# Local attention steps between the input projection's matmuls, linear attention levels on half of the queries, and its norm sums as columns

## The reference, cut to what matters

```
attn = sliding_window_attention(aq, ak, av, sinks) * silu(ag)   # 8 query heads, 2 key heads, 64 wide, window 128
rkv  = rkv + (shift(rkv) - rkv) * mu_rkv                        # token mix, 6 tiles of 128 channels
rwkv = rwkv7(h, r, k, v, ...) * silu(rg)                        # 4 heads
# linear attention, 4 heads, 32 keys and 64 values wide; b = cumulative sum of the gate's logs
A[i,j] = sum_d q[i,d] k[j,d] exp(b[i,d] - b[j,d])   for j <= i
o      = A @ v + (q exp(b)) @ S
gla    = o * rsqrt(mean(o*o) + 1e-5) * norm_w * silu(gg)
```

## Time and profile before

| | |
|---|---|
| median of 3 runs (lowest, highest) | 2209.52 us (2199.64, 2214.57) |
| the profiled execution | 2206.71 us, its span 2204.7 us |
| TensorE busy, share of the span | 1927.6 us, 87% |
| VectorE busy | 1241.7 us, 56% |
| ScalarE busy | 638.6 us, 29% |
| GpSimd busy | 103.1 us, 5% |
| mean granted TensorE clock | 0.930 |
| HBM read | 146.59 MB, 67 GB/s over the span |
| the projection's 208 matmuls (L1453) | 181.7 us busy |

### The profile page before, as it was taken

One profiled execution on the slowest core, in us unless ns is written; L12 is line 12 of the kernel. 1 busy time (PEld: TensorE's weight loads), 2 busy tenths in 40 slices (PEclk: granted clock), 3 DMA queues, 4 the chain that ended last, 5 costly groups with the idle time before them and its releaser, 6 DMA issues.

```text
span 2204.7 us, 34977 instructions
## 1 busy us (share of the span) xinstructions
PE 1927.6 (87%) x14866; PEld 1658.0 (75%) x14866; DVE 1241.7 (56%) x2291; ACT 638.6 (29%) x1219; POOL 103.1 (5%) x54
## 2 busy tenths in 40 slices
PE   3999663499799887899999999798889999999997
PEld 1444443395499744799999999498866799999996
DVE  6110247641465566478787334689466558878523
ACT  1011331221321355232222222311167632222221
POOL 0000000020000000000000001033300000000000
PEclk8999875799899988799999999899999999999998
DMA  7333100001044200133332333143200022323331
GB/s 296 119 124 96 38 0 1 0 4 39 29 120 132 58 1 1 39 97 94 89 94 89 96 96 106 29 115 103 73 20 1 1 94 89 94 89 96 89 102 60
DMA packets 51002, 160.68 MB, mean 73 GB/s; under 512 B 7968, under 2 KB 8864, under 8 KB 50720
## 3 DMA queue, kind: packets, MB, share of 16 engines
q1 hardware_dynamic: 43360, 147.62, 21.8%
q10 hardware_dynamic: 7488, 10.82, 1.9%
HBM read 146.59 MB, written 2.10 MB: 67 GB/s over the span
## 4 chain that ended last, share of the span: by engine, by line
PE 78%; DVE 17%; issue 2%; ACT 1%; DMA 1%; ACTq 0%; SPq 0%; DVEq 0%
PE banks L460 16%; PE banks L461 16%; PE banks L462 16%; PE banks L1453 8%; PE banks L1577 3%; PE banks L1739 3%; PE banks L527 2%; DVE arena L1354 2%; DVE top L1353 2%; PE banks L581 1%; PE banks L505 1%; PE banks L517 1%; PE banks L1515 1%; PE banks L553 1%; DVE stat L1117 1%
## 5 line engine op out<-in xcount | busy, mean ns | idle before, releaser
L460 PE MATMUL banks<-hn_hi,w_hi 128*128 128x264 f32 x2288 | 659.3, 288 | 30.5 <-DVE hn_lo L1033 14.2
L461 PE MATMUL banks<-hn_lo,w_hi 128*128 128x264 f32 x2288 | 654.4, 286 | 0.0
L462 PE MATMUL banks<-hn_hi,w_lo 128*128 128x264 f32 x2288 | 653.8, 286 | 0.0
L799 ACT ACTIVATE w_hi<-raw 128x1024 fp32r<-128x1024 f32 x207 | 219.5, 1062 | 895.7 <-PE banks L462 861.3
L460 PEld LDWEIGHTS banks<-hn_hi,w_hi 128*128 128x128 f32 x2288 | 437.1, 191 | 34.9 <-issue 20.3
L461 PEld LDWEIGHTS banks<-hn_lo,w_hi 128*128 128x128 f32 x2288 | 437.7, 191 | 0.1
L462 PEld LDWEIGHTS banks<-hn_hi,w_lo 128*128 128x128 f32 x2288 | 435.3, 190 | 0.0
L1027 DVE TENSOR_TENSOR w_lo<-raw,w_hi 128x1024 fp32r<-128x1024 f32 x181 | 221.6, 1225 | 199.6 <-ACT w_hi L799 199.6
L460 PE MATMUL banks<-a_hi,w_hi 128*128 128x264 f32 x704 | 199.6, 284 | 1.6 <-DVE u_in L1240 1.6
L461 PE MATMUL banks<-a_lo,w_hi 128*128 128x264 f32 x704 | 200.5, 285 | 0.0
L1453 PE MATMUL banks<-hn_raw,ring 128*128 128x512 f32 x416 | 181.7, 598 | 20.6 <-DVE hn_raw L1984 20.6
(11 more groups left out here) (336 smaller groups left out, 2750.9 us busy)
## 6 DMA issues: line engine op xcount, KB each, us to landing
raw<-in_weights SPq DMA_DIRECT2D x207, 512.0 KB, 3.6
ring<-in_weights SPq DMA_DIRECT2D x50, 512.0 KB, 4.2
arena<-arena ACTq DMA_DIRECT2D x144, 66.0 KB, 2.2
arena<-in_gate_w SPq DMA_DIRECT2D x8, 512.0 KB, 4.6
h<-in_xT SPq DMA_DIRECT2D x2, 1024.0 KB, 10.7
out_t<-h SPq DMA_DIRECT2D x4, 512.0 KB, 2.8
arena<-in_alibi SPq DMA_DIRECT2D x1, 1024.0 KB, 5.3
arena<-in_cosT ACTq DMA_DIRECT2D x2, 264.0 KB, 3.2
```

What stands on the lines that cost most here:

```text
L460: mm(o, w[0][:, j, :], x[0][:, k, t], start=first, stop=False)
L461: mm(o, w[0][:, j, :], x[1][:, k, t], start=False, stop=False)
L462: ins_ = mm(o, w[1][:, j, :], x[0][:, k, t], start=False, stop=last)
L799: nc.scalar.activation(w_hi[:, j % SPLIT, :], raw[:, j % RAW, :], ACT.Copy).then_inc(S["w_hi_done"], 1)
```

## The change

It has three parts.

1. **Order of the projection.** The groups come as low-rank inputs, local attention's q, k, v and gate, then the other fourteen: r, k, v of the third mixer (6), q, k, v of linear attention (4), and two pairs of gates. The first 17 items (`ALONE`) use banks as before; the last 14 alternate between banks 4 and 5. Attention starts after item 16, and its 16 steps (transposes(u), scores(u+1), values(u-1)) are issued behind every seventh of the 112 matmuls. ScalarE evacuates the late items between its attention parts, VectorE does a token mix in steps 2 to 7 and a gate sum in steps 8 to 15. The queries are held once; the scores are two products over 64 rows in two banks, the values two products 64 columns wide, and the gate one instruction. The identity and the alibi table are loaded earlier, the casts of two constants come after attention, the remaining gates are copied and get their silu during linear attention's levels.
2. **Levels.** The distances are formed by two instructions of half the length, queries are scaled and multiplied in the later halves alone (256 instead of 512 columns), and one masked copy takes two heads of 256 elements each. The masks come as bytes from memory in the packed order, and the diagonal has its own.
3. **Norm.** Sums, root and reciprocal of linear attention work on 8 columns per tile, and are spread by `spread_columns`.

```diff
-        for g in range(8, N_IN1):
+        for g in range(8, 12):
             in1(g + 5, g)
...
             for s in range(2):
-                last = mm(psum[:, u % 3, s * w:(s + 1) * w], qz1[:, g, s, n * P:(n + 1) * P], k1[:, lo:lo + w], start=True, stop=True)
+                r = slice(64 * s, 64 * s + 64)
+                last = mm(psum[:, 2 * (u % 2) + s, 0:w], q1[r, g, n * P:(n + 1) * P], k1[r, lo:lo + w], start=True, stop=True)
...
+            for b in range(blocks):
+                for s in range(2):
+                    r = slice(64 * s, 64 * s + 64)
+                    last = mm(psum[r, 7, 0:P], v1tok[:, max(0, n - 1) + b, r],
                               pt1[:, u % 2, (s * blocks + b) * P:(s * blocks + b + 1) * P], start=b == 0, stop=b == blocks - 1)
...
+        def s1_step(u):
+            s1_transposes(u)
+            if u + 1 < 16:
+                s1_scores(u + 1)
+            if u >= 1:
+                s1_values(u - 1)
+        s1_scores(0)
+        for g in range(12, N_IN1):
+            def between(k, at=8 * (g - 12)):
+                if (at + k) % 7 == 6:
+                    s1_step((at + k) // 7)
+            in1(g + 5, g, between=between)
         s1_values(15)
...
         s1_exp(0)
         for u in range(16):
+            while 8 * taken + 7 <= 7 * u + 6 and taken < 14:
+                late(taken)
+                taken += 1
+            s1_copy(u)
             if u + 1 < 16:
                 s1_exp(u + 1)
...
         for u in range(16):
+            s1_normalise(u)
             if u + 1 < 16:
                 s1_max(u + 1)
-            s1_normalise(u)
             if u >= 1:
                 s1_gate(u - 1)
+            if 2 <= u < 8:
+                token_mix(u - 2)
+            elif u >= 8:
+                gate_sum(u - 8)
         s1_gate(15)
+        ve.wait_ge(S["consts_in"], 16 * 9)
+        V.tensor_copy(identb[:, :], ident[:, :])
...
-            j = n - S_IN1 - 16
+            j = n - S_IN1 - 20
...
+            V.tensor_tensor(g_half(e, lv, 1), b[:, :, s:2 * s], edge, ALU.subtract)
+            V.tensor_tensor(g_half(e, lv, 0), edge, b[:, :, 0:s], ALU.subtract).then_inc(S["g_diff"], 1)
...
+                    if lv < 7:
+                        o = slice(c * 64, (c + 1) * 64)
+                        last = mm(psum[:, hd, o], g_kl[r, lv % 2, t], g_ql[r, lv % 2, o], start=True, stop=True)
...
+            for hd in range(0, 4, 2):
+                ve.wait_ge(S["g_score"], 4 * lv + hd + 2)
+                if lv < 7:
+                    at = g_at[:, hd:hd + 2, :].rearrange("p h (n a w) -> p h n a w", a=2, w=1 << lv)[:, :, :, 1, :]
+                    shape = [P, 2, T1 // 2]
+                    V.copy_predicated(at, glamask[:, lv:lv + 1, :].to_broadcast(shape).rearrange("p h (n w) -> p h n w", w=1 << lv),
+                                      psum[:, hd:hd + 2, 0:T1 // 2].rearrange("p h (n w) -> p h n w", w=1 << lv)).then_inc(S["g_taken"], 1)
...
+        A(rgate, rgate, ACT.Silu)
+        A(ggate, ggate, ACT.Silu)
...
-            mm(bank(2 + j), bones, g_o_sq(j), start=True, stop=True).then_inc(S["g_osum"], 1)
+            column_sums(psum[:, 2 + j, 0:8], g_o_sq(j)).then_inc(S["g_osum"], 1)
+        for j in range(2):
+            pe.wait_ge(S["g_oinv"], j + 1)
+            spread_columns(bank(4 + j), g_cols[:, 8 * j:8 * j + 8]).then_inc(S["g_orow"], 1)
...
+            V.reciprocal(g_cols[:, 8 * j:8 * j + 8], g_cols[:, 8 * j:8 * j + 8]).then_inc(S["g_oinv"], 1)
```

More of the change, by code:

```diff
@@ L171, in build @@
     att_at = c1.at
-    qz1 = c1.take(4, 2, T1)
+    q1 = c1.take(4, T1)
     k1 = c1.take(T1)
     v1 = c1.take(T1)
+    p1 = c1.take(2, 2, 256)
+    pt1 = c1.take(2, 4 * P)
+    v1tok = c1.take(4, P)
     tail_at = c1.at
@@ L179, in build @@
     dmix = c1.take(T1)
-    mask_in = c1.take(8, P)
     cond = c1.take(D)
@@ L192, in build @@
     g_d = cg.take(2, T1)
-    g_ql = cg.take(2, T1)
+    g_ql = cg.take(2, T1 // 2)
+    g_sq = cg.take(2, T1)
+    g_cols = cg.take(16)
     g_kl = cg.take(2, T1)
@@ L336, in build, with in_bank @@
     ITEMS = 31
+    ALONE = 17
+    def in_bank(item):
+        return bank(item % 8 if item < ALONE else 4 + (item - ALONE) % 2)
     def zb_d(k):
@@ L1452, in in1 @@
                     pe.wait_ge(S["hn_ready"], k + 1)
-                last = mm(bank(item % 8), w[:, k, :], rhs(k), start=k == 0, stop=k == KT - 1 and g > 0)
-            last.then_inc(S["slot_used"], 1)
+                last = mm(in_bank(item), w[:, k, :], rhs(k), start=k == 0, stop=k == KT - 1 and g > 0)
+                if k == KT - 1:
+                    last.then_inc(S["slot_used"], 1)
+                if between:
+                    between(k)
         in1(0, 0)
@@ L1577, in both_heads @@
                 last = mm(out(s), lhs[r], rhs[r], start=start, stop=stop)
[L1578 to L1586, removed]
-            for n in range(4):
-                for s in range(2):
-                    last = mm(out[64 * s:64 * s + 64, n * P:(n + 1) * P], src[:, 2 * n + s:2 * n + s + 1].to_broadcast([P, 64]), ident[:, :],
-                              start=True, stop=True)
             return last
@@ L1800, in _ @@
         evac(glow, 1).then_inc(done, 1)
-        for j in range(6):
+        for j in range(4):
             take(2 + j)
-            evac(zb[:, j, 1:T1 + 1], 2 + j).then_inc(done, 1)
+            evac(q1[:, j, :], 2 + j).then_inc(done, 1)
+        take(6)
+        evac(k1, 6).then_inc(done, 1)
+        take(7)
+        evac(v1, 7).then_inc(done, 1)
         for j in range(2):
@@ L1863, in s1_copy, with late @@
             A(pt1[:, u % 2, 0:w], psum[:, 6, 0:w], ACT.Copy).then_inc(S["s1_pt"], 1)
+        LATE = ([(zb[:, j, 1:T1 + 1], 1.0) for j in range(6)] + [(gq, 32.0 ** -0.5), (gk, 1.0)] + [(gv[:, j, :], 1.0) for j in range(2)]
+                + [(rgate[:, j, :], 1.0) for j in range(2)] + [(ggate[:, j, :], 1.0) for j in range(2)])
+        def late(j):
+            dst, f = LATE[j]
+            take(ALONE + j)
+            evac(dst, ALONE + j, scale=f).then_inc(done, 1)
+        taken = 0
         s1_exp(0)
         for u in range(16):
+            while 8 * taken + 7 <= 7 * u + 6 and taken < 14:
+                late(taken)
+                taken += 1
+            s1_copy(u)
             if u + 1 < 16:
                 s1_exp(u + 1)
-            s1_copy(u)
+        while taken < 14:
+            late(taken)
+            taken += 1
         act.wait_ge(S["g_cum"], 1)
@@ L1992, in _, with token_mix @@
         ve.wait_ge(S["zeroed"], 1)
-        for j in range(6):
-            ve.wait_ge(S["in1_evac"], 3 + j)
+        def token_mix(j):
+            ve.wait_ge(S["in1_evac"], ALONE + 1 + j)
             st.link(V.tensor_tensor(dmix, zb[:, j, 0:T1], zb[:, j, 1:T1 + 1], ALU.subtract))
@@ L2356, in _constants @@
         lvl.append(-1.0 * (((j % 64) // (2 * s) == q64 // (2 * s)) & (j % (2 * s) < s) & (q64 % (2 * s) >= s)))
-    gla = [((j // (2 * s) == q // (2 * s)) & (j % (2 * s) < s) & (q % (2 * s) >= s)) for s in (1 << np.arange(7))]
-    gla.append(j == q)
+    gla = []
+    for n in range(7):
+        s = 1 << n
+        late = q.reshape(-1, 2, s)[:, 1, :].reshape(1, -1)
+        gla.append(np.tile((j // (2 * s) == late // (2 * s)) & (j % (2 * s) < s), (1, 4)))
+    gla = np.stack(gla, axis=1)
     gblock = (i[:, None] // 32 == np.arange(256)[None, :] // 64)
```

154 lines of the change are left out of this document (68 added, 86 removed).

## The result

The changed kernel takes 2134.39 us (median of 4 runs, 2127.97 to 2136.79) against 2211.51 before: ratio 0.9656, 95% interval 0.9614 to 0.9699. The forecast was 2130, within 2112 to 2154. The profiled execution has a span of 2125.9 us, against 2204.7.

What follows compares the result with a forecast made beforehand. Projection was taken as bound by TensorE's work, local attention by latency, the levels by VectorE. Gains of 60.5 (attention inside projection), 11.7 (levels) and 5.0 (norm), together 77.2, off 2206.71 gave about 2130 us, range 2112 to 2154.

Steps and rivals of the forecast that it cites:

- The start: Start of attention inside the projection: front part ends at 144.7; hand-over 1.8 and a wait of 0.4 make 146.9 us.
- The step: Attention's TensorE work behind every seventh matmul: 2.0 us per full step, 1.2 per half-size one, 28.8 us for all 16.
- It is wrong if the exposed loads exceed 0.4 us a step: Sign against the forecast in the attention steps: changes of array shape, taken at 0.13 each, costing over 0.4 us a step.
- The cover claimed for the round trip: Attention steps: seven matmuls (6.0 us) and values (0.55) hide the 3.5 us from scores to normalised probabilities, 3 us slack.
- The tail: From the last matmul's end to linear attention's scan: 3.75 us, 0.65 of it casts and sums; scan at 273.6.
- The levels: Linear attention levels on the later halves: a period of 4.28 us against 5.87; gain 11.7 us, bounds 11 and 17.
- Strided access I cost at nothing: Masked copies in the levels: no cost for strided access; at half the copy's speed, 8.5 us lost over seven levels.
- The norm: Linear attention's norm with sums as columns: 7.9 us instead of 12.9; gain 5.0 us, bounds 4 and 6.
- 1 (lower level): Mixed projection and attention stage: TensorE's clock falls to its lower level throughout, +125 us, 2255; chance 0.03.
- 2 (gate transfers set the step): Attention's gate steps: a transfer handshake makes eight of them 10.7 us instead of 8.0, +21 us, 2151; chance 0.10.
- 3 (no pairing, dear changes): Attention steps: paired products do not overlap and every change of array shape costs, +16.6 us, 2146; chance 0.13.
- 4 (all it says): Attention and levels: pairs perfect (-10.6 us) and level products halved (-5.3), 2114 us; chance 0.08.

Runs made afterwards that it cites:

- experiment 4: The changed kernel with the value products 128 columns wide again and two gate instructions; 2143.16 us, one run.
- experiment 3: The changed kernel with all 112 late matmuls first and the 16 attention steps behind them, without overlap; 2196.59 us, ratio to before 0.9931.
- experiment 5: The changed kernel with attention steps alternately 4 and 10 matmuls apart, and only the first gate-weight slice loaded and used; 2131.55 us, one run.
- experiment 6: The changed kernel with attention steps alternately 2 and 12 matmuls apart, and only the first gate-weight slice loaded and used; 2142.90 us, one run.
- experiment 7: The changed kernel with masked copies writing densely in levels 0 and 1, with gaps between runs of 1, 2 and 4 in levels 3, 4 and 6; 2138.36 us.
- experiment 8: The changed kernel with the even levels' products loading 64 weight columns instead of 128, odd levels as they are; 2130.66 us.
- experiment 2: The kernel before with the new levels and norm only, projection and attention left old; 2197.62 us, ratio 0.9928.
- experiment 9: The changed kernel with gate sums one step earlier, and constant casts and two small sums moved to the third mixer; 2133.65 us, ratio to before 0.9653.
- experiment 10: The changed kernel with GpSimd's two memsets waiting for VectorE's first result after the scan; 2130.68 us, one run.
- experiment 11: The changed kernel with one extra 128x512 matmul into an unused bank behind the products of each of levels 0 to 6; 2132.85 us, ratio 0.9647.

## Why the prediction was right

**The start.** Forecast: first transposes after 146.9 + 6.0 = 152.9. Measured 152.78, with a wait of 0.3 for the table loads' chain (0.4 forecast).

**The step.** Forecast 2.0 us of attention work, measured 1.86 (7.87 less seven matmuls of 0.859); a step of half size was forecast at 1.2 and takes 1.2. The sum is right, but its two terms are both off, in opposite directions, and that is luck. The products were forecast at 1.6 and take 1.3: transposes 0.44, scores 0.43, values 0.44, the pairs running wholly beside each other. The changes of shape were forecast at 0.4 and take 0.54, by the table of experiment 4. "It is wrong if the exposed loads exceed 0.4 us a step" thus did come true. Both terms rest on the earlier trace rows, and both readings of these rows were wrong. The 2.25 us of the norm-spreading rows began at the lower level and ended at the upper, as the clock column of these two stretches shows:

```profile
423.60:425.00 1.40, 1.40 (x21) 1.33 (x22) 0.00 (x0) 0.00 (x0) 0.00 (x0) 0.75 0.00 0
425.00:426.00 1.00, 0.92 (x18) 0.68 (x14) 0.03 (x1) 0.00 (x0) 0.00 (x0) 1.00 0.00 0
```

At 1.00 a pair there starts 0.11 us behind the last, 0.055 an instruction and not 0.07. And the first pair of rows, said to show no cost of a change, does hold one: the groups of four 32-row products start 0.21 us apart, the last of them at 383.68, the transposes 0.37 behind it. The average of 0.066 an instruction had hidden it. The cover claimed for the round trip (3.5 us) was the claim that carried the forecast; experiments 3, 5 and 6 show it from three sides.

**The tail.** Forecast 3.75 us from the end of the last matmul to the scan, measured 4.9. Of this, casts and sums had 0.65 and took 2.2, because a memset on GpSimd begins with the same gate. I had named what moves onto VectorE's path, but not what another engine does at that moment. The cheaper steps hid the mistake: scan forecast 273.6, measured 273.01.

**The levels.** This term was mis-sized: 11.7 forecast, 9.4 measured. The term that failed was "Strided access I cost at nothing", and the sign named for it, masked copies over 0.7 us, did appear: 1.21 us in two levels. Experiment 7 puts it in the destination: gaps between runs of 1 and 2 elements double the copy, which is 1.2 us in each of two levels, 2.3 together. The bound stated for it (8.5 us in seven levels) had the price of one level right and the number of levels wrong. TensorE's part was right in kind and nearly in size: 2.06 us, not 1.06, with the weight load as its floor, as experiment 8 shows.

**The norm.** 5.0 forecast, 5.9 measured. From 316 to 335 us the changed kernel ran at the upper level. Over the twelve traces with this code the norm takes 6.9 to 8.9 us, a gain of 4 to 6, which are the bounds that the prediction gave; 5.9 is the favourable end, and experiment 2 has 4.2.

**The rest.** The third mixer became 1.4 us longer and the untouched second block 3.7 us shorter. From the output projection's start to the end fourteen traces give 1684 to 1693 us with the same code. I had given it no term, and rightly; but differences of a few us between single runs say nothing.

**The sum.** The medians differ by 77.1 us, the forecast gain was 77.2. That is closer than the forecast deserves: the interval is 67 to 85, levels and norm were off by 2.3 and 0.9 in opposite directions, and the forecast started from a profiled execution 4.8 us below the median of before, which is about the distance from 2130 to 2134.

**The rivals.** 1 (lower level): refuted, 1.00 throughout. 2 (gate transfers set the step): refuted, the step's chain is TensorE alone. 3 (no pairing, dear changes): refuted in its first half by experiment 4; the changes cost 0.15 to 0.20, between the 0.13 taken and its 0.3. 4 (all it says): the pairs were perfect, but the gaps between shapes remained, and the level products did not halve.

## What to carry to other kernels

A chain of small steps that goes round three engines costs its round trip, not its work: here steps of 5.9 us cost 1.9 us each when matmuls longer than the round trip stood between them, and the same steps without that cover won nothing. Measure the round trip first, and place just enough independent work in it (here 4 us were enough and 2.5 were not). After such a change read the seam behind it again: what had idle time to run in, on every engine, now stands on the path.

## What the runs showed of the hardware

- A masked copy of 512 fp32 elements into a destination with gaps takes 1.21 us when the runs are 1 or 2 elements and 0.63 to 0.66 when they are 4 to 64; into a dense destination, with mask and source still in rows of 1 or 2, it takes 0.67 (experiment 7 and the changed kernel).
- A cast of 128 columns on VectorE took 1.91 us beside a memset on GpSimd and 0.22 without it; the scan beside the memset kept its 1.22 us (experiments 9 and 10).
- At the lower level, products over 32 rows with 64 moving columns took 2.06 us for 32 instructions with 128 weight columns and 1.21 with 64 (experiment 8).
- Each change of the array's shape cost 0.15 to 0.20 us at the upper level, about half of it ahead of the first instruction of the new shape and the rest behind it (changed kernel and experiment 4). Pairs of 64-column products started 0.11 us apart, as single 128-column ones did.
- TensorE at 29.45 of 34 us busy stayed at a clock of 0.50 (experiment 11), its lower level of 1.2 GHz.
- The old attention code ran at a mean clock of 0.70 in the kernel before and 0.57 in experiment 2, and took 7.2 us longer there.
